# RWKV chunk inverse: five of its six doubling steps on packed 32x32 diagonal blocks, and the two gate products of a head pair in two PSUM banks

## The reference

```python
def step(state, inp):
    r_t, w_t, k_t, v_t, a_t, b_t = inp
    sa = jnp.einsum('bhij,bhj->bhi', state, a_t)
    state = (state * w_t[:, :, None, :] + sa[..., None] * b_t[:, :, None, :]
             + v_t[..., None] * k_t[:, :, None, :])
    return state, jnp.einsum('bhij,bhj->bhi', state, r_t)
```

## Time and profile before

| what | value |
|---|---|
| median of the runs | 3332.87 us (3327.38 to 3342.9, three runs) |
| the profiled execution's own time | 3329.62 us |
| span of the profile, first to last instruction | 3327.8 us |
| mean granted TensorE clock | 0.992 of 2.4 GHz |
| instructions in the profile | 52710 |
| PE, DVE, ACT, POOL busy | 3242.5, 1774.2, 1247.7, 193.2 us |

### The profile page before, as it was taken

The page is one execution under the profiler, slowest core; times in us unless marked ns, Lnnn a source line. Parts: engine busy times, 40 slices in busy tenths (PEclk is TensorE's granted clock), DMA queues, the critical chain, the costliest instruction groups (busy, mean ns, idle before and its releaser), DMA issues. The chain is left out here.

```text
span 3327.8 us, 52710 instructions
## 1 busy us (share of the span) xinstructions
PE 3242.5 (97%) x22179; PEld 2664.4 (80%) x22179; DVE 1774.2 (53%) x2970; ACT 1247.7 (37%) x1967; POOL 193.2 (6%) x156
## 2 busy tenths in 40 slices
PE   7999999999999999989999999999999999999999
PEld 6877777777777787867788888888888888888887
DVE  5235555545555455363436777433656566655832
ACT  4124343433333332242325666323334344443421
POOL 1000000001001111100000111010000000000000
PEclk9999999999999999999999999999999999999999
DMA  7433333331212134332442122443332233322552
GB/s 234 114 82 87 86 98 92 87 109 48 62 54 83 57 113 146 95 114 76 111 110 80 45 58 86 130 145 108 89 89 89 76 95 94 96 89 76 165 143 85
DMA packets 492528, 324.30 MB, mean 97 GB/s; under 512 B 27130, under 2 KB 448605, under 8 KB 491782
## 3 DMA queue, kind: packets, MB, share of 16 engines
q1 hardware_dynamic: 492294, 320.94, 33.3%
HBM read 276.05 MB, written 44.85 MB: 96 GB/s over the span
## 5 line engine op out<-in xcount | busy, mean ns | idle before, releaser
L534 PE MATMUL PS<-XH,WHT 128*128 128x512 f32 (+1 forms) x2224 | 897.7, 404 | 7.1 <-DVE AR L1031 2.1
L522 DVE TENSOR_TENSOR WLT<-AR,WHT 128x1024 fp32r<-128x1024 f32 (+1 forms) x430 | 527.3, 1231 | 667.2 <-ACT WHT L516 666.8
L536 PE MATMUL PS<-XH,WLT 128*128 128x512 f32 (+1 forms) x2224 | 872.6, 392 | 0.0
L516 ACT ACTIVATE WHT<-AR 128x1024 fp32r<-128x1024 f32 (+1 forms) x430 | 446.9, 1042 | 646.6 <-PE PS L536 483.5
L535 PE MATMUL PS<-XL,WHT 128*128 128x512 f32 (+1 forms) x1712 | 671.2, 392 | 0.0
L534 PEld LDWEIGHTS PS<-XH,WHT 128*128 128x128 f32 (+1 forms) x2224 | 417.5, 188 | 109.2 <-issue 10.8
L536 PEld LDWEIGHTS PS<-XH,WLT 128*128 128x128 f32 (+1 forms) x2224 | 417.7, 188 | 96.2
L535 PE MATMUL PS<-ARR,WHT 128*128 128x512 f32 x1024 | 404.6, 395 | 0.0
L535 PEld LDWEIGHTS PS<-XL,WHT 128*128 128x128 f32 (+1 forms) x1712 | 321.7, 188 | 71.7 <-issue 4.6
L535 PEld LDWEIGHTS PS<-ARR,WHT 128*128 128x128 f32 x1024 | 192.4, 188 | 40.4 <-issue 0.2
L534 PE MATMUL PS<-XL,WHT 128*128 128x512 f32 x512 | 203.3, 397 | 0.1
(11 more groups left out here) (487 smaller groups left out, 5336.5 us busy)
## 6 DMA issues: line engine op xcount, KB each, us to landing
AR<-b_w_in SPq DMA_DIRECT2D x128, 512.0 KB, 4.0
AR<-w_in SPq DMA_DIRECT2D x122, 512.0 KB, 4.1
AR<-a_w_in SPq DMA_DIRECT2D x48, 512.0 KB, 4.4
AR<-w_out SPq DMA_DIRECT2D x32, 512.0 KB, 4.8
AR<-a_w_out SPq DMA_DIRECT2D x32, 512.0 KB, 4.0
AR<-b_w_out SPq DMA_DIRECT2D x32, 512.0 KB, 4.1
proj_scratch<-AR SPq DMA_DIRECT2D x33, 256.0 KB, 2.0
AR<-a_w_kv_up SPq DMA_DIRECT2D x32, 256.0 KB, 3.7
```

Source lines behind the costliest of these rows:

```text
L516: self.nc.scalar.activation(self.shaped(self.high, n), self.shaped(self.raw, n), ACT.Copy).then_inc(self.s_high, 1)
L522: self.nc.vector.tensor_tensor(self.shaped(self.low, n), self.shaped(self.raw, n), f32(self.shaped(self.high, n)), ALU.subtract).then_inc( ...
L534: mm(out, wh, xh[k0 + c], start=(start and c == 0), stop=False)
L536: last = mm(out, wl, xh[k0 + c], start=False, stop=(stop and c == nk - 1))
```

## The change

1. The steps up to block size 16 touch only the two 32x32 blocks on the diagonal of each 64x64 matrix. The new kernel keeps these blocks alone: partition 64e + 32b + r holds row r of block b of head e. The tiles `LOT`, X, T and its transpose (`TD`) are 32 columns wide where they were 64. `GD` holds the diagonal blocks of L transposed.
2. `products` and `sums` of steps 1 to 4 issue one 32x32 matmul for each chunk, block and head, in the order chunk (then product or transpose), block, head: 16 and 32 matmuls a half where there were 8 and 16.
3. Step 5 (size 32) makes the one block off the diagonal from the two on it: 8 matmuls of 32x32 a half for X, taken from `GB` with no mask (the POOL operation of step 5 goes), and 16 a half for the sums: X times T, and T's second diagonal block times the identity, which brings it to the right place. The result goes to `TF`, the full upper 64x64 factor, by a DVE copy; `diagonal` on DVE fills the first block of `TF` from `TD` and zeroes the rest.
4. `lower` computes only diagonal blocks, of L and of L transposed: 64 matmuls of 32 columns (64 partitions deep) in place of 16 of 64x64.
5. DVE: `GD` is copied out of PSUM, one masking of both (128x512), one addition of the identity (128x512). Additions in the steps are 128x256 in place of 128x512; two scalings of 128x128 are new.
6. Products and sums of a half share one bank (bank h) at different columns. This leaves banks 2 and 3 free, and the two gate products go there, both after step 2, with no wait between them.

```diff
-    X = take(T).rearrange("p (c f) -> p c f", f=CH)
+    X, GD = (take(T // 2).rearrange("p (c f) -> p c f", f=SB) for _ in range(2))
...
-    TT = take(2 * T).rearrange("p (h j c f) -> p h j c f", h=2, j=2, f=CH)
+    TD = take(T).rearrange("p (j c f) -> p j c f", j=2, f=SB)
+    TF = take(T).rearrange("p (c j f) -> p c j f", j=2, f=SB)
...
+    def sub(e, b):
+        return slice(64 * e + SB * b, 64 * e + SB * b + SB)
...
+    def at(c, j=0):
+        return slice((j * HC + c) * SB, (j * HC + c + 1) * SB)
...
             for i in range(NPAIR):
-                for l in levels:
+                for l in levels[:-1]:
...
-                    S.did(nc.gpsimd.tensor_tensor(LOT[l % 2], GB[:, :, 0, :], lev(l + 1), ALU.mult), "pool", f"lot{l}")
+                    S.did(nc.gpsimd.tensor_tensor(LOT[l % 2], GD, lev(l + 1), ALU.mult), "pool", f"lot{l}")
...
-                    N.wait(pe, i - 1, "act.tokA")
-                else:
-                    N.wait(pe, i, "act.sgw")
-                N.did(mm(B[6][:, :], W2[rows(e), :], TW[rows(e), :], start=True, stop=True), "pe", ("zw", "za")[e])
+                N.did(mm(B[2 + e][:, :], W2[rows(e), :], TW[rows(e), :], start=True, stop=True), "pe", ("zw", "za")[e])
...
             def lower(i):
                 S.wait(pe, i - 1, "dve.qt")
-                G.did(each(range(NCH), lambda c, e: mm(B[0][rows(e), tok(c)], AR[rows(e), 0, tok(c)], SQN[rows(e), tok(c)], start=True, stop=True)), "pe", "lm")
+                for j in range(2):
+                    for c in range(NCH):
+                        for b in blocks:
+                            for e in heads:
+                                x, y = AR[rows(e), 0, stok(c, b)], SQN[rows(e), stok(c, b)]
+                                last = mm(B[0][sub(e, b), j * T // 2 + c * SB:j * T // 2 + (c + 1) * SB], (x, y)[j], (y, x)[j], start=True, stop=True)
+                G.did(last, "pe", "lm")
...
-                    S.did(each(range(HC), lambda c, e: mm(B[h][rows(e), tok(c)], LOT[l % 2][rows(e), HC * h + c, :], TT[rows(e), h, 0, c, :], start=True, stop=True)), "pe", f"x{h}{l}")
+                    if l < LAST:
+                        S.wait(pe, i, f"pool.lot{l}")
+                        for c in range(HC):
+                            for b in blocks:
+                                for e in heads:
+                                    last = mm(B[h][sub(e, b), at(c)], LOT[l % 2][sub(e, b), HC * h + c, :], TD[sub(e, b), 0, HC * h + c, :], start=True, stop=True)
+                    else:
+                        last = each(range(HC), lambda c, e: mm(B[h][sub(e, 1), at(c)], GB[sub(e, 0), HC * h + c, 0, SB:CH], TD[sub(e, 0), 0, HC * h + c, :], start=True, stop=True))
...
+                    if l < LAST:
+                        for c in range(HC):
+                            for j in range(2):
+                                for b in blocks:
+                                    for e in heads:
+                                        x, t = X[sub(e, b), HC * h + c, :], TD[sub(e, b), 1, HC * h + c, :]
+                                        last = mm(B[h][sub(e, b), SB * HC + SB * (HC * j + c):SB * HC + SB * (HC * j + c + 1)], (t, x)[j], (x, t)[j], start=True, stop=True)
+                    else:
+                        for c in range(HC):
+                            for b in blocks:
+                                for e in heads:
+                                    x, t = X[sub(e, 1), HC * h + c, :], TD[sub(e, 1), 1, HC * h + c, :]
+                                    last = mm(B[h][sub(e, b), at(c, 2)], (x, C("eye32")[sub(e, 1), :])[b], t, start=True, stop=True)
...
-                    if l in (2, 3) and more:
-                        decays(i + 1, l - 2)
+                    if l == 2 and more:
+                        decays(i + 1, 0)
+                        decays(i + 1, 1)
...
-                        S.did(A(X[:, HC * h:HC * h + HC, :], B[h][:, 0:HC * CH].rearrange("p (c f) -> p c f", f=CH), ACT.Copy), "act", f"xc{h}{l}")
+                        S.did(A(X[:, HC * h:HC * h + HC, :], B[h][:, 0:HC * SB].rearrange("p (c f) -> p c f", f=SB), ACT.Copy), "act", f"xc{h}{l}")
...
-                G.did(TTn(full, full, eye(2 * NCH), ALU.add), "dve", "t0b")
+                G.did(TTn(full, full, C("eye32").unsqueeze(1).broadcast_to([P, 2 * NCH, SB]), ALU.add), "dve", "t0b")
...
+            def diagonal(i):
+                for h in halves:
+                    S.wait(dve, i, f"dve.ta{h}{LAST - 1}")
+                    cs = slice(HC * h, HC * h + HC)
+                    S.did(TS(TF[:, cs, 0, :], TD[:, 1, cs, :], C("upper"), None, ALU.mult), "dve", f"tf{h}")
```

More of the change, by code:

```diff
@@ L41 @@
 LEVELS = [1, 2, 4, 8, 16, 32]
+SB = 32
 GN_EPS = 64e-5
@@ L103, in constants @@
     lev = []
-    for m in LEVELS:
+    r, t = i[:, None] % SB, np.arange(SB)[None]
+    for m in LEVELS[:-1]:
         low = (r // (2 * m) == t // (2 * m)) & (r % (2 * m) >= m) & (t % (2 * m) < m)
@@ L1212, in rwkv @@
     heads, halves, levels = range(2), range(2), range(1, NL)
+    blocks = range(2)
+    LAST = NL - 1
     A_, B_, K_, V_ = 1, 2, 3, 4
@@ L1485, in sums @@
                     S.wait(pe, i, f"act.xc{h}{l}")
-                    def one(c, e, n=1):
-                        x, tt = X[rows(e), HC * h + c, :], TT[rows(e), h, 1, c, :]
-                        if n:
-                            return mm(B[2 + h][rows(e), tok(HC + c)], x, tt, start=True, stop=True)
-                        return mm(B[2 + h][rows(e), tok(c)], tt, x, start=True, stop=True)
-                    S.did((both if l < NL - 1 else each)(range(HC), one), "pe", f"t{h}{l}")
+                    if l < LAST:
[11 more added lines that the diff above has]
+                                    last = mm(B[h][sub(e, b), at(c, 2)], (x, C("eye32")[sub(e, 1), :])[b], t, start=True, stop=True)
+                    S.did(last, "pe", f"t{h}{l}")
             def value_scores(i):
@@ L1503, in solved @@
                 for h in halves:
-                    S.wait(pe, i, f"dve.ta{h}{NL - 1}")
-                    S.did(each(range(HC), lambda c, e: mm(B[h][rows(e), blk(c)], TT[rows(e), h, 1, c, :], TOK[rows(e), 0:2, HC * h + c, :], start=True, stop=True)), "pe", f"pt{h}")
+                    S.wait(pe, i, f"dve.ta{h}{LAST}")
+                    S.did(each(range(HC), lambda c, e: mm(B[h][rows(e), blk(c)], TF[rows(e), HC * h + c, :, :], TOK[rows(e), 0:2, HC * h + c, :], start=True, stop=True)), "pe", f"pt{h}")
             def increments(i):
@@ L1918, in gram @@
-                G.wait(dve, i, "dve.tt0a")
-                full = TT.rearrange("p h j c f -> p (h j c) f")
-                G.did(TTn(full, full, eye(2 * NCH), ALU.add), "dve", "t0b")
+                S.wait(dve, i - 1, f"pool.lot{LAST - 1}", "pe.pt1")
+                both = B[0][:, :].rearrange("p (j c f) -> p j c f", j=2, f=SB)
+                G.did(V.tensor_copy(GD, both[:, 1, :, :]), "dve", "gd")
+                m = C("lev", 0, 2 * SB).rearrange("p (j f) -> p j f", f=SB).unsqueeze(2).broadcast_to([P, 2, NCH, SB])
@@ L1922, in level @@
+                G.did(TTn(TD, both, m, ALU.mult), "dve", "t0a")
+                G.wait(dve, i, "dve.t0a")
+                full = TD.rearrange("p j c f -> p (j c) f")
+                G.did(TTn(full, full, C("eye32").unsqueeze(1).broadcast_to([P, 2 * NCH, SB]), ALU.add), "dve", "t0b")
             def level(i, h, l):
                 S.wait(dve, i, f"pe.t{h}{l}")
[L1924 to L1927 removed]
@@ L2036, in _ @@
                         evac(tile(i, 0))
+                    if l == LAST - 1:
+                        diagonal(i)
                     if tail and l == 4:
```

51 lines of the change are left out of this document (24 added, 27 removed).

## The result

The changed kernel takes 3353.77 us, median of six runs (3346.26 to 3357.77). The kernel before, beside it, takes 3333.46 (3327.38 to 3342.9). The ratio is 1.006 with a 95% interval of 1.0046 to 1.0075: some 20 us slower, where 32 us faster was forecast. The profiled execution of the changed kernel took 3356.32 us, 26.7 more than that of before, so the traces explain 26.7 us.

The account below looks back on a forecast made before the run. PE's matmul time was taken as the bound: 4.1 us less a pair, 32.8 for eight, minus corrections of 1.6 and 1.5, about 30 less than 3329.6, 3299.6, stated as 3301; range 3284 to 3352.

Parts of the forecast that it names:

- The slot: Steps 1 to 4 on PE: four 32x32 matmuls side by side in 33 ns, 6.3 us a pair.
- two abreast: Rival: only two small matmuls overlap, 16.4 us a pair against 14.1; 21 us slower, 3352; chance 0.13.
- one at a time: Rival: no small matmuls overlap, 33 ns each, 32.7 us a pair, 149 us slower; chance 0.01.
- Step 5 and `lower`: PE terms priced two abreast for shared rows: step 5 1.6 us, `lower` 2.1 us a pair.
- More overlap than booked: Rival: blocks of one head overlap in `lower` and step 5 too, 1.8 us less a pair, 3286; chance 0.05.
- PSUM: Rule weighed: different row tiles cannot access one bank simultaneously; trace contradicts it for two tiles, nothing shown for four.
- matmuls cannot be supplied faster: Rival: small-matmul issue limited; at 29.4 ns a record 121 us slower, 3450, chance 0.07; 3350 to 3420, chance 0.04.
- supply near 14 ns a record: Rival, shared with three abreast: gain and loss on the small matmuls cancel, 3320 to 3345; chance 0.12.
- whether hundreds in a row can be is open: Doubt within the supply rival: short bursts of matmuls are dense, but long ones unproven; PE gains 4096 matmul records.
- The clock: Granted clock in the last two pairs: one stretch more or less at 1.2 GHz moves the time by some us.
- Other engines: Nothing booked: additions shrink from 0.69 towards 0.42 us under cover, POOL masks halve, moved gate products worth nothing.
- Two slips in the sums: Prediction's arithmetic: 64 columns at 1.03 ns called some 60 ns; 3299.6, 3.3 under the median, called 3301.

Follow-up runs that it names:

- experiment 6: Changed kernel with the two gate products back at their old places (after steps 2 and 3), both in bank 6: 3353.19 us, ratio 1.0053.
- experiment 1: Changed kernel with every matmul of `lower` issued twice, same results: 3397.46 us, ratio 1.0198.
- experiments 4: Changed kernel with piece 1 (12 dense matmuls) moved into step 1 and every piece halved, six matmuls ahead of each half's `sums`: 3345.62 us.
- 5: Changed kernel with `lower` in 64x64 matmuls, dense piece 1 moved into step 1, and pieces halved ahead of each half's `sums`: 3329.62 us, again 3333.07.
- 7: Changed kernel plus 216 unused 128x512 matmuls (49 us) behind each half's `sums` of steps 1 to 3, pairs 0 to 5: 3384.08 us.
- 3: Changed kernel with piece 1 (12 dense matmuls) moved from ahead of step 1 to between its `products` and `sums`: 3356.53 us, ratio 1.0061.
- 10: Changed kernel with 64x64 `lower` and pieces halved in steps 2 to 5, piece 1 whole and ahead of step 1: 3348.80 us, ratio 1.0044.

## Why the prediction was wrong

- **The slot, right.** 35 ns against the 33 forecast, four abreast, by the timeline and without pauses. The rivals "two abreast" and "one at a time" are out. The first lies at 3352, nearly the measured time, and is still wrong: its mechanism would show 1.2 us for `products` (32 slots of 33 ns and the 0.13), and they take 0.68. A matching total is no proof of a mechanism.
- **Step 5 and `lower`, mis-sized in the good direction.** 2.1 us was booked for `lower` for its shared rows; it takes 1.1. "More overlap than booked" (0.05) was true of the array.
- **PSUM, right.** Four row strips write one bank at 8.7 ns a record. The Trainium skill (TensorEngine Tiling, "Gotcha 1: PSUM Pressure") says that different row tiles cannot; that is contradicted here for four tiles as it was for two. Each of the tiles writes partitions of its own, and row tiles that write the same partitions were not run.
- **The failed step: the supply of instructions.** The rival "matmuls cannot be supplied faster" was priced as a pace between one matmul and the next, 29.4 or 25 ns, and given 0.11; "supply near 14 ns a record" had 0.12. Both looked for a limit that holds at every moment, and the evidence against them, two starts within 0.05 us (PE is busy for only the last 0.01 of them), was right for that question. The real limit is one of volume: 4.4 ns an instruction up to the end of the block that has come, and 13.7 on average in a burst that lasts. The runs show 34.5 us of it, at the ends of blocks of 256 instructions. The sentence that named the doubt, "whether hundreds in a row can be is open", was the place to stop: 176 packets of 16 KB stood on the page, and in the trace of the kernel before no two of them start closer than 3.65 us in this part, 14.3 ns an instruction, which a burst at 4.4 undercuts by far. The Trainium skill's floor (TensorE: Matmul & The Clock Gate, "Wait — 56ns, not 53.3ns?"), 25 ns from start to start, does not hold between strips: 8.7 was measured. Another page of the Trainium skill bears on this (Runtime: NRT & Kernel Launch, "Instruction fetch mechanics"): blocks of 256 instructions, whose fetching is called mostly hidden, because dispatch is slower than the refill. The block size agrees with the 16 KB packets and with the places of the waits. That it is hidden does not: 34.5 us here.
- **The clock, wrong as well.** "A smaller matter" of some us was up to 38: PE worked for 93.7 us at 1.2 GHz, 18.2 before. It was read from the kernel before, where PE is busy for 65.4 of 68.6 us, and assumed to stay.
- **Other engines, right.** The additions (L1957) take 0.42 us, no wait of `products` for them beyond 0.2 us in all; the gate products are worth nothing that can be told (experiment 6). Nothing was booked for L1537, which now waits 1.5 us for the last step's copy on DVE (L1959).
- **Two slips in the sums** change nothing: 64 columns at 1.03 ns are 66 ns and not some 60, and 3299.6 with the 3.3 us under the median is 3303 and not 3301.

**What stays open.** The supply is shown by its own packets, by the places of the waits and by experiment 1. Why the clock falls more often is not. Of the 20 stretches at 1.2 GHz, 11 begin during a wait for instructions or within 2.8 us of its end. The other nine follow waits in the recurrence, seven of them its pauses of 1.0 to 1.1 us, which are the same as before, where the clock mostly held. Time at 1.2 GHz goes along with the waits for instructions in most versions (experiments 4, 5, 7), but not in all (3 has fewer waits and more time at 1.2 GHz, 10 fewer and as much). Whether the pauses, or the bursts of small matmuls as such, bring it down was not parted, and so neither was how much of the 38 us is the supply's in the second place. Nor was it tried how the fetching goes when it meets a large transfer: the longest wait, 4.5 us at 747 to 751.5, lies in its first half in a stretch in which the DMA engines were full, and the packet that ends it starts at 748.88, when they are about to come free.

## What to carry to other kernels

Before cutting matmuls into smaller ones, count instructions and not only array time: PE got 256 instructions per 3.5 us here, and started to fetch a block at most some 300 ahead, so a run of several hundred that each take less than 13.7 ns is likely to stall, however well they pack. Read the page's line of the instruction queue, and compare the densest stretch's time per instruction with that supply. Where dense bursts are wanted, put long matmuls of other work between them, and spend few instructions ahead of them; here that won back the 20 us that the packing had lost, and no more.

## What was not expected of the hardware

- Matmuls of one head that read the same rows but write different columns overlap as fully as those of different rows: 8.5 ns a record in `lower`, 8.7 in the steps.
- Packets of PE's instructions, mostly 0.9 to 1.4 us each, start no closer than 3.31 us apart in the changed kernel's part even when the DMA engines are otherwise idle, and PE goes on 2.2 to 2.8 us after a packet's start. None starts more than 301 of PE's records ahead of its block in any kernel here.
- 49 us of dense array work cost 30 us, while waits for instructions and time at 1.2 GHz shrank: adding work to PE can be partly free on an engine that looks 96% busy.
